# A two-block transformer on one core: attentions moved behind the recurrence's levels, and a first tile that does not wait for its norm

## The reference, cut to what matters

```python
h = rms_norm(x, attn_norm[l])                      # x * factor(token) * gain(channel)
proj = h @ w_in[l]
(aq, ak, av, iq, ik, iw, bq, bf, bi, bg, cq, ckv, ckpe, gate_logits) = jnp.split(proj, ...)
# branch a: attention over the top-k keys that an indexer picks
logits = einsum('bthd,bsd->bths', iq, ik)
score = einsum('bths,bth->bts', relu(logits), iw) * idx_scale     # causal, then top_k
o_a = softmax(aq k_sel * scale + bias) v_sel
# branch b: gated recurrence over chunks of 64 tokens (state decays by f)
o_b = rms_norm(recurrence(bq, bf, bi), out_gain) * silu(bg)
# branch c: latent attention, causal, with rope on q_pe and k_pe (= ckpe)
o_c = softmax((q_nope k_nope + rope(q_pe) rope(k_pe)) * scale) v_c
mixed = g_a * (o_a @ w_up_a) + g_b * (o_b @ w_up_b) + g_c * (o_c @ w_up_c)   # g = sigmoid(gate_logits)
x = x + mixed @ w_out
x = x + swiglu(rms_norm(x, ffn_norm))
...                                                # the second layer, not touched
```

## Time and profile before

| | |
|---|---|
| median of three runs | 1048.18 us (1047.95 to 1049.42) |
| the profiled execution | 1047.96 us |
| its span | 1046.2 us |
| TensorE busy | 1037.4 us, 99% |
| VectorE, ScalarE, GpSimd busy | 734.0, 581.3, 79.3 us |
| granted TensorE clock, mean | 1.00 |

### The profile page before, as it was taken

The page is one execution under the profiler, slowest core; times in us unless marked ns, Lnnn a source line. Parts: engine busy times, 40 slices in busy tenths (PEclk is TensorE's granted clock), DMA queues, the critical chain, the costliest instruction groups (busy, mean ns, idle before and its releaser), DMA issues.

```text
span 1046.2 us, 22213 instructions
## 1 busy us (share of the span) xinstructions
PE 1037.4 (99%) x8760; PEld 1010.5 (97%) x8760; DVE 734.0 (70%) x1092; ACT 581.3 (56%) x885; POOL 79.3 (8%) x92
## 2 busy tenths in 40 slices
PE   9999999999999999999999999999999999999998
PEld 7999998999999999999999999898899999999998
DVE  6899998647866666657666567567977866665666
ACT  4556655576565554556554445455666665454554
POOL 0000000002310000111000001041001300000110
PEclk9999999999999999999999999999999999999999
DMA  6456533245555554665655456564335555554563
GB/s 220 148 182 215 196 103 133 97 158 197 173 197 200 200 195 138 207 200 190 218 186 194 155 192 218 181 205 174 127 122 202 193 189 185 197 210 147 195 222 121
DMA packets 32444, 187.81 MB, mean 180 GB/s; under 512 B 3832, under 2 KB 7552, under 8 KB 14720
## 3 DMA queue, kind: packets, MB, share of 16 engines
q1 hardware_dynamic: 31472, 185.58, 51.0%
q0 software_dynamic: 416, 1.06, 0.4%
q10 hardware_dynamic: 496, 0.33, 0.1%
HBM read 184.98 MB, written 1.06 MB: 178 GB/s over the span
## 4 chain that ended last, share of the span: by engine, by line
PE 87%; DVE 7%; issue 1%; ACT 0%; DVEq 0%
PE acc L685 83%; PE area_a L685 2%; DVE wlo L1581 2%; PE area_t L685 2%; DVE score L1808 1%; PE area_t L952 1%; DVE work L1821 0%; DVE st L1819 0%; DVE mask L1783 0%; DVE h L1980 0%; DVE s_sum L2138 0%; DVE st L1768 0%; DVE he L1876 0%; DVE he L1877 0%; DVE pp L1617 0%
## 5 line engine op out<-in xcount | busy, mean ns | idle before, releaser
L685 PE MATMUL acc<-hs,whi 128*128 128x256 f32 x3584 | 617.8, 278 | 1.7 <-DVE wlo L1581 1.2
L685 PEld LDWEIGHTS acc<-hs,whi 128*128 128x128 f32 x3584 | 539.3, 187 | 8.5 <-issue 4.6
L685 PE MATMUL acc<-hs,wlo 128*128 128x256 f32 x1792 | 495.0, 276 | 0.0
L1184 ACT ACTIVATE whi<-raw 128x1024 fp32r<-128x1024 f32 (+3 forms) x379 | 357.0, 978 | 169.0 <-PE acc L685 151.2
L1581 DVE TENSOR_TENSOR wlo<-raw,whi 128x1024 fp32r<-128x1024 f32 (+4 forms) x259 | 273.8, 1098 | 99.5 <-ACT whi L1184 98.3
L685 PEld LDWEIGHTS acc<-hs,wlo 128*128 128x128 f32 x1792 | 335.6, 187 | 0.2
L685 PE MATMUL acc<-hid,whi 128*128 128x256 f32 x1056 | 179.7, 276 | 0.0
L685 PEld LDWEIGHTS acc<-hid,whi 128*128 128x128 f32 x1056 | 158.9, 188 | 0.0
L685 PE MATMUL acc<-hid,wlo 128*128 128x256 f32 x528 | 145.7, 276 | 0.0
L1669 DVE TENSOR_TENSOR wlo<-raw,whi 128x1024 fp32r<-128x1024 f32 x120 | 141.1, 1218 | 4.1 <-ACT whi L1184 4.1
L1682 DVE TENSOR_TENSOR hbuf<-acc,sbuf 128x256 f32<-128x256 f32 x66 | 28.0, 425 | 116.8 <-PE acc L685 112.3
(11 more groups left out here) (314 smaller groups left out, 1022.2 us busy)
## 6 DMA issues: line engine op xcount, KB each, us to landing
raw<-in_w_gu SPq DMA_DIRECT2D x66, 1024.0 KB, 4.7
raw<-in_w_dn SPq DMA_DIRECT2D x48, 704.0 KB, 4.1
raw<-in_w_up SPq DMA_DIRECT2D x10, 1024.0 KB, 4.8
raw<-in_w_gates1b SPq DMA_DIRECT2D x8, 1024.0 KB, 4.9
raw<-in_w_out SPq DMA_DIRECT2D x8, 1024.0 KB, 4.8
raw<-in_w_qk SPq DMA_DIRECT2D x8, 1024.0 KB, 4.8
raw<-in_w_gates SPq DMA_DIRECT2D x8, 1024.0 KB, 4.8
raw<-in_w_projT_b SPq DMA_DIRECT2D x7, 1024.0 KB, 4.8
```

The source lines that it names most:

```text
L685: return nc.tensor.matmul(out, w, m, start=start, stop=stop, skip_group_check=True)
L1184: return nc.scalar.activation(out, in_, f, **kw)
```

## The change: the order of both attentions and the levels, and the input of the first five blocks

- **The opening's input.** A new array `hu = x * gain`, without the token factor, is split on ScalarE (`hu_high`) and VectorE (`hu_low`), and tiles 0 to 2 read it. The factor of the keys is multiplied in by GpSimd (two 64 x 256 multiplies), that of the queries by ScalarE's relu, whose scale becomes a column per token: `column0` makes it with two one-column matmuls and two small VectorE instructions. The normed `hs` is still made, in four pairs (`hs01` to `hs67`). `keep_warm` has 2 matmuls in place of 6.
- **Transfers.** The copies that double the keys move from ScalarE's queue to SyncE's, behind the load of tile 3, where SyncE waits for GpSimd. The constants' two transfers move behind the load of tile 2.
- **Order.** Levels and their matmuls run in rows 15 to 23, back to back. Both attentions stand behind them, in rows 24 to 34. Tiles 21 to 24 are now gates, 25 to 27 `q_c` and `kv_c`. The masks, the parts of `top` and `mla_norm`, `rope_k`, `decay` move by a row or several.

```diff
-    add("w_qb", 2, 9 * P, 6 * P)
-    add("w_kvb", 1, full, full // 2)
-    add("w_gates1b", 8, full, full // 2)
+    add("w_gates1b", 4, full, full // 2)
+    add("w_qb", 2, 9 * P, 6 * P)
+    add("w_kvb", 1, full, full // 2)
+    tiles.extend(("w_gates1b", i, full, full // 2) for i in range(4, 8))
...
-    work("distances mask0 drel norm0 bias0 H1 L1")
...
-    work("12a 12b rope_k H14 L14 decay_xa decay_b")
+    work("distances mask0 drel norm0 bound0 rest0 bias0 H1a L1a")
+    work("0a hs01 H1b L1b 0b H2 L2 hs23")
+    work("1a 1b H3a L3a hs45 H3b hs67 L3b bounde")
...
+    work("8a 8b rope_k H10 top_d0 L10")
...
-    work("24a dsa_o 24b mla_s0 lev6 H26 L26")
...
-    work("30a 30b hgrn_v mla_o H32 L32")
...
+    work("23a 23b level_x8 level_m8 lev7 far H25 L25")
+    work("24a dsa_s0 24b H26 dsa_e0 L26 dsa_p0")
...
+    work("32a 32b H34 hgrn_gate hgrn_v L34")
+    work("33a hgrn_h 33b H35 gate_sigmoid1_1 mla_o L35")
...
-                    load(a[name][i], g % 2, n, 2 * g - 2)
+                    load(a[name][i], g % 2, n, {2: 1, 3: 3}.get(g, 2 * g - 2))
+                if g == 2:
+                    sp.dma_start(con[:, f:e], a["consts"][:, f:e]).then_inc(S("con_loaded"), 16)
+                    sp.dma_start(con[:, e:], a["consts"][:, e:]).then_inc(S("masks_loaded"), 16)
+                if g == 3:
+                    sp.wait_ge(S("keys_scaled"), 1)
+                    sp.dma_start(kpe[ROPE:P, :], kpe[0:ROPE, :]).then_inc(S("keys_doubled"), 16)
+                    sp.dma_start(ik[0:ROPE, :], ik[ROPE:P, :]).then_inc(S("keys_doubled"), 16)
...
+            def opening_tile():
...
+                    for k in range(KD):
+                        if b == 0:
+                            pe.wait_ge(S("hu_lo"), k + 1)
...
-                        keep_warm(BLOCKS["kik"], 6)
+                        keep_warm(BLOCKS["kik"], 2)
...
+            def hu_high(chunks):
+                for k in chunks:
+                    fn(hu[:, k, 0:T], x[:, k, :], ACT.Copy, scale=late_gain("norm0", k)).then_inc(S("hu_hi"), 1)
...
+                    act.wait_ge(S("column_scaled"), 1)
                     fn(relu_l[:, 4 * hg:4 * hg + 4, 0:keys(tt)], area_a[:, :, 0:keys(tt)], ACT.Relu,
-                       scale=IDX_D ** -0.5 * IDX_H ** -0.5).then_inc(S("a_freed"), 1)
+                       scale=st[:, 108 + tt:109 + tt]).then_inc(S("a_freed"), 1)
...
+            def normed_pair(chunks):
+                dve.wait_ge(S("t_freed"), TURN_T["norm0"] + 1)
+                for k in chunks:
+                    v.scalar_tensor_tensor(tmp[:, k % 4, :], x[:, k, :], late_gain("norm0", k), xr[:],
                                            ALU.mult, ALU.mult).then_inc(S("h_value"), 1)
+                for k in chunks:
+                    hs_low("norm0", k, tmp[:, k % 4, :])
...
+            pool.wait_ge(S("copied"), LEFT_PSUM[BLOCKS["kik"]][1])
+            pool.wait_ge(S("t_freed"), TURN_T["norm0"] + 1)
+            nc.gpsimd.tensor_tensor(kpe[0:ROPE, :], kpe[0:ROPE, :], xr[0:ROPE, :], ALU.mult)
+            nc.gpsimd.tensor_tensor(ik[ROPE:P, :], ik[ROPE:P, :], xr[ROPE:P, :], ALU.mult).then_inc(S("keys_scaled"), 1)
```

More of the change, by code:

```diff
@@ L205, in work @@
                 o.append(("step", item))
-    work("distances mask0 drel norm0 bias0 H1 L1")
[L208 to L219, removed]
-    work("12a 12b rope_k H14 L14 decay_xa decay_b")
-    work("13a 13b H15 L15 decay_u")
-    work("14a 14b H16 decay_xb L16 decay_c decay_d")
+    work("distances mask0 drel norm0 bound0 rest0 bias0 H1a L1a")
+    work("0a hs01 H1b L1b 0b H2 L2 hs23")
+    work("1a 1b H3a L3a hs45 H3b hs67 L3b bounde")
+    work("2a 2b column0 H4 mask1 3a L4 3b bias1 H5 mask2")
+    work("4a idx00 4b H6 bias2 L5 mask3 idx01 tables")
+    work("5a bias3 L6 tables2 idx10 5b H7 mask4 top_a0 bias4 idx11 L7")
+    work("6a bound1 mask5 6b H8 bias5 top_b0 L8")
+    work("7a 7b H9 top_c0 L9")
+    work("8a 8b rope_k H10 top_d0 L10")
+    work("9a 9b input_squares H11 top_a1 L11")
+    work("10a 10b H12 mla_norm L12 top_b1 decay_a")
+    work("11a 11b H13 L13 mla_normed mla_low")
+    work("12a 12b H14 decay_xa L14 top_c1")
+    work("13a 13b H15 L15 decay_b decay_u")
+    work("14a 14b H16 decay_xb L16 top_d1 decay_c decay_d")
     work("15a 15b decay_xc level_m0 H17 L17 level_e1")
@@ L225, in order_of_work @@
     work("17a 17b level_e2 level_x2 level_m2 lev1 level_e3 H19 L19")
[L226 to L231, removed]
-    work("24a dsa_o 24b mla_s0 lev6 H26 L26")
[L233 to L237, removed]
-    work("30a 30b hgrn_v mla_o H32 L32")
[L239 to L242, removed]
+    work("18a 18b level_x3 level_m3 lev2 level_e4 H20 L20")
+    work("19a 19b level_x4 level_m4 lev3 level_e5 H21 L21")
+    work("20a 20b level_x5 level_m5 lev4 level_e6 H22 L22")
+    work("21a 21b level_x6 level_m6 lev5 level_e7 H23 L23")
+    work("22a 22b level_x7 level_m7 lev6 level_e8 H24 L24")
+    work("23a 23b level_x8 level_m8 lev7 far H25 L25")
+    work("24a dsa_s0 24b H26 dsa_e0 L26 dsa_p0")
+    work("25a 25b H27 L27 dsa_s1")
+    work("26a dsa_t0 26b H28 L28")
+    work("27a rope_q dsa_e1 27b dsa_p1 H29 L29")
+    work("28a mla_s0 dsa_t1 28b H30 mla_e0 L30 mla_p0")
+    work("29a hgrn_o mla_t0 29b H31 hgrn_n L31")
+    work("30a dsa_o 30b H32 mla_s1 L32")
+    work("31a mla_e1 31b H33 gate_sigmoid1_0 mla_p1 L33")
+    work("32a mla_t1 32b H34 hgrn_gate hgrn_v L34")
+    work("33a hgrn_h 33b H35 gate_sigmoid1_1 mla_o L35")
+    work("34a 34b H36 gate_sigmoid1_2 L36")
     work("35a 35b H37 L37")
@@ L1390, in step @@
                     norm(name)
+                elif name == "rest0":
+                    rest_of_opening()
+                elif name in ("hs01", "hs23", "hs45", "hs67"):
+                    hs_high((int(name[2]), int(name[3])))
                 elif name == "tables":
@@ L1484, in step @@
                         load_set(SIGMOIDS)
[L1485 removed]
+                    last = (("gates1a", 7), ("gates1b", 7), ("gates1c", 7))[b] if first_block else \
                         ("gates2", 8 * b + 7)
@@ L1553, in _ @@
                     split_high(what, 1)
-                elif kind in ("low", "low_first", "low_second"):
+                elif kind == "high_first":
+                    split_high(what, 0)
+                elif kind == "high_second":
+                    split_high(what, 1)
+                elif kind.startswith("low"):
                     pass
@@ L1881, in step @@
                     norm(name)
+                elif name == "rest0":
+                    rest_of_opening()
+                elif name in ("hs01", "hs23", "hs45", "hs67"):
+                    normed_pair((int(name[2]), int(name[3])))
+                elif name == "column0":
+                    factor_columns()
                 elif name == "tables":
                     tables()
+                elif name == "tables2":
+                    dve.wait_ge(S("sines"), 2)
+                    link(v.tensor_scalar(sin[:], sin[:], con[:, C_SIGN:C_SIGN + 1], None, ALU.mult))
                 elif name == "distances":
```

137 lines of the change are left out of this document (78 added, 59 removed).

## The result

The changed kernel takes 1061.38 us (median of 5 runs, 1060.30 to 1063.22), the kernel before 1048.18 beside it (1047.87 to 1049.42). The ratio is 1.0125, with an interval of 1.0111 to 1.0139: 13.2 us slower, where the forecast was 5.9 slower and its range ended at 1057.6. The profiled execution took 1061.38 us, its span is 1059.5, and the mean granted clock 0.997 where it was 1.00.

What follows compares the result with a forecast made beforehand. The prediction took TensorE to bound the kernel, with VectorE almost as full in the first 121 us. It summed +3.1 - 1.7 + 4.5 = +5.9 on 1047.96 to 1053.9 us, range 1048.9 to 1057.6.

Steps and rivals of the forecast that it cites:

- The term ahead of `lev0`: Up to `lev0`: VectorE's list ends late, TensorE waits 4.5 us, the start's gain is eaten and 3.1 us are lost.
- The opening: First weight tiles: without the token factor TensorE starts 2.4 us sooner, and tile 1 ends 3.4 us sooner.
- The indexer's sums: VectorE from tile 3's low part: 27.3 us of work, sums end at 53.5, `idx11` starts at 54.5 after TensorE waits 1.5.
- GpSimd's two multiplies ... hidden: Key factor near the start: two multiplies of 0.8 us each, hidden because the keys' first use stands four tiles later.
- From `rope_k` to `level_m0`: VectorE's stretch before the levels: starts at 73.3, takes 50.6 us, `level_m0` ends at 123.9, 3.0 to 3.1 later.
- the list of its later stretch: VectorE's old work from `top_d0` to `level_m0`: 56.41 us, less low parts 4.6 and waits 2.6, gives 49.2.
- Rival 3: After `lev0`'s wait: TensorE falls back to its slow first-matmul pace, 2.4 us on top, 1056.3 in all; chance 0.11.
- From `lev0` to the up tiles: Later part: three old waits go (1.7 us), four new ones come, together 5.8, taken as 4.5.
- all four waits: TensorE waits at `osplit_b` (1.9 to 2.1), the mix behind `gate_sigmoid1_1` (1.4), `dsa_o` (1.5) and `far` (1.0).
- The removal of 1.7: Attentions' steps: three old TensorE waits, 1.7 us, go because `mla_s0`, `dsa_t1` and `rope_q` now stand elsewhere.
- Rivals 1 and 2: First: VectorE's stretch does not bind, no new waits, 1042.7, chance 0.07; second: only that stretch costs, 1049.4, chance 0.12.
- Rival 4: Early transfers: constants now ahead of tile 3's load make it late, 1.3 us on the forecast, 1055.2; chance 0.04.

Runs made afterwards that it cites:

- e4_squares_on_pe: The changed kernel with branch c's squares summed by three more TensorE matmuls instead of GpSimd's adds: 1060.59 us, ratio 1.0125.
- e2_top_d1_late: The changed kernel with `top_d1` moved from ahead of the recurrence's scan to behind `far`: 1056.22 us, ratio 1.0073.

## Why the prediction was right in direction and wrong in size

Two steps of the sum failed. The term ahead of `lev0` was put at +3.1 and measured +6.1; and the clock behind the wait there, which had no term in the sum, took 2.8 us.

- **The opening** was right in its start, 14.13 against 14.0. The end of tile 1, forecast at 25.3, came at 25.67: TensorE began tile 1's second half at 22.80, behind a wait for its low part, where its pace of 0.34 us a chunk gives 22.45.
- **The indexer's sums** were 0.8 short (51.64 + 2.68 = 54.32 against 53.5), and all but 0.2 of that came in with tile 3's low part at 26.83 instead of 26.2. (At 28.66, where the prediction puts tile 3's low part in the kernel before, tile 1 ends on TensorE and `mask2` starts on VectorE; that low part stands at 31.17. Both are in either list, so the 27.3 holds.) "GpSimd's two multiplies ... hidden" left a cost out: they were priced as time of GpSimd alone. Beside them VectorE's `tmp` pair takes 1.84 us; the next pair, without them, 0.88. In the changed kernel's timeline:

```profile
18.06 0.85 POOL L2313 TENSOR_TENSOR kpe<-kpe,xr 64x256 f32<-64x256 f32 x1 [17.60 <-ACT ik L1215]
18.24 1.84 DVE L1817 SCALAR_TENSOR_TENSOR tmp<-x,vec,xr 128x256 f32<-128x256 f32 x2
18.97 0.82 POOL L2314 TENSOR_TENSOR ik<-ik,xr 64x256 f32<-64x256 f32 x1
...
23.86 0.88 DVE L1817 SCALAR_TENSOR_TENSOR tmp<-x,vec,xr 128x256 f32<-128x256 f32 x2
```

  How much of tile 3's delay comes from this pair's 0.96 was not tried. In the timeline VectorE stands idle for 1.19 us ahead of that low part and waits for ScalarE's high part, which stands behind the eviction of tile 1's last block. So the pair can have made tile 3 late by no more than tile 1's end came late, 0.4 of the 0.6 us.
- **From `rope_k` to `level_m0`** is the term that failed most: mechanism and place were right, the size was +3.1 and measured +6.1. 1.7 came in with `rope_k` (74.96 for 73.3; 1.2 of it with `idx11`, 55.66 for 54.5), 1.4 from the list (52.0 for 50.6), of which the score's sums are 1.2. The step said that VectorE has there "the list of its later stretch" less two low parts and the waits; it took durations of before as they stood, where GpSimd had other neighbours. `e4_squares_on_pe` showed the neighbour, `e2_top_d1_late` the binding list. That the wait came out right (4.3 against 4.5) although `lev0` was 3 us late is luck: TensorE also arrived 3.3 later, at 122.7 instead of 119.4. 1.7 of that is the late start, and 1.05 a wait that was not forecast, at 87.89 for tile 11's low part, which stands behind the slowed sums.
- **Rival 3**, the clock behind the wait, had a chance of 0.11 and no place in the sum. It happened, at a price of 2.8 us where 2.4 was worked out, and in some executions a second time behind `idx11`. The prediction expected a 4.5 us wait, over six times the longest then seen with a clock of 1.00 (0.7), so the rows spoke neither for nor against a fall; it gave the fall a low chance all the same. The Trainium skill's page "TensorE: Matmul & The Clock Gate", section "Part 1: The HAM clock gate (the "warmup" mystery)", whose rule the prediction quoted, agrees with this trace: granted 0.52 and 0.63 behind the 4.3 us wait, 1.00 when it was filled.
- **From `lev0` to the up tiles**: all four waits came, 1.8, 1.2, 1.4 and 1.0 for 1.9 to 2.1, 1.4, 1.5 and 1.0. The sum of 5.8 was right within 0.4. Taking 0.3 off each made it 4.5 (4.6 by its own figures) and was wrong: what had been seen on two small waits of before did not hold for these four. The removal of 1.7 held.
- **Rivals 1 and 2** fell with the 4.3 at `lev0` and the tail's 5.4. **Rival 4**: tile 3 was 0.6 late, half its price; whether the constants took part was not tried.

By terms: +3.0 at `lev0`, +2.8 of clock and +0.6 to +0.9 in the tail account for 6.4 to 6.7 of the 7.4 us between the two spans' difference and the forecast.

## What to carry to other kernels

When TensorE starts sooner on in-order engines, ask first whether the list of the engine that releases its next dependent step gets shorter too; here 2.2 us of head start turned into a wait, and with VectorE's list cut 0.6 us of it reached `lev0`. A wait of a few us on TensorE is not priced by its length alone: add what the following work costs at the lower clock (2.8 us here behind 4.3 of waiting), or keep it filled. Durations taken from a trace hold for the neighbours they had: work that moves beside GpSimd is to be priced again.
